# Running two attention mixers inside the input projection of block 2 of a two-block transformer kernel

## The reference

```python
def token_mixer_2(h, w_in, w_out, lam_params, subln_gain, layer):
    proj = h @ w_in                                   # (512,1024) @ (1024,3072)
    qa, ka, va, qb, kb, vb, qc, kc, vc = jnp.split(proj, idx, axis=-1)
    o_a = dilated_attention(...)        # 6 heads of 64: softmax(q k^T + bias) v
    o_b = differential_attention(...)   # 4 heads: (softmax(q1 k1^T + b) - lam softmax(q2 k2^T + b)) v, q/k of 32
    o_b = rmsnorm(o_b, subln_gain) * (1.0 - lam_init)
    o_c = stick_breaking_attention(...) # 6 heads
    mixed = jnp.concatenate([from_heads(o_a), from_heads(o_b), from_heads(o_c)], axis=-1)
    return mixed @ w_out
```

## Time and profile before

| what | value |
|---|---|
| median of 3 runs | 3406.91 us |
| range of the runs | 3401.34 to 3408.74 us |
| span of the profiled execution | 3402.8 us |
| PE busy | 3190.5 us (94%) |
| projection to end of attention with z(0), z(1), layer 0 | 1688.59 to 1905.28 us |
| the same, layer 1 | 2724.97 to 2940.14 us |

### The profile page before, as it was taken

How to read it: one execution, slowest core, us unless ns; L and a number is a source line. 1 busy time by engine, 2 the same in 40 slices (tenths; PEclk the granted TensorE clock), 3 DMA queues, 4 the chain that set the end, 5 groups by cost and what they waited for, 6 DMA issues and landing times.

```text
span 3402.8 us, 61162 instructions
## 1 busy us (share of the span) xinstructions
PE 3190.5 (94%) x26588; PEld 2518.9 (74%) x26588; DVE 1893.5 (56%) x2803; ACT 1251.0 (37%) x2065; POOL 179.8 (5%) x168
## 2 busy tenths in 40 slices
PE   7989789999997889999998899999999999899999
PEld 6866678865532335998886579988998886579987
DVE  4457566565221116884426568845885424658853
ACT  3227434321100003543324654534443324654432
POOL 0013222131000000000000000000000000000000
PEclk9999899999999999999999999999999999999999
DMA  7140000224999994333430023332332331013322
GB/s 264 50 161 11 3 4 3 71 80 173 408 413 421 421 421 162 103 97 112 136 118 13 1 87 100 100 112 87 112 102 99 133 119 38 1 62 112 100 93 87
DMA packets 179765, 441.65 MB, mean 130 GB/s; under 512 B 7602, under 2 KB 107692, under 8 KB 154924
## 3 DMA queue, kind: packets, MB, share of 16 engines
q1 hardware_dynamic: 179500, 437.74, 34.8%
HBM read 435.62 MB, written 2.10 MB: 129 GB/s over the span
## 4 chain that ended last, share of the span: by engine, by line
PE 72%; DMA 8%; DVE 7%; ACT 4%; issue 3%; POOL 0%; SPq 0%; ACTq 0%; DVEq 0%; POOLq 0%
PE banks L349 8%; PE banks L3616 7%; PE banks L3619 7%; PE banks L3618 7%; PE banks L2733 5%; PE banks L3737 4%; PE banks L3738 4%; PE banks L3736 4%; DMA ring<-in_exp_w_down 3%; DMA ring<-in_exp_w_gate 3%; DMA ring<-in_exp_w_up 1%; PE banks L973 1%; PE banks L957 1%; PE banks L911 1%; PE banks L393 1%
## 5 line engine op out<-in xcount | busy, mean ns | idle before, releaser
L2733 PE MATMUL banks<-ring,arena 128*64 128x512 f32 x1120 | 263.0, 606 | 37.8 <-DMA ring<-in_exp_w_gate 13.8
L3738 PE MATMUL banks<-tail_r,hid_r 128*128 128x512 f32 x704 | 279.7, 397 | 0.0
L3737 PE MATMUL banks<-ring_r,two_r 128*128 128x512 f32 x640 | 254.1, 397 | 0.0
L3736 PE MATMUL banks<-tail_r,two_r 128*128 128x512 f32 x640 | 250.7, 392 | 0.0
L2733 PEld LDWEIGHTS banks<-ring,arena 128*64 128x64 f32 x1120 | 86.4, 139 | 201.1 <-issue 186.8
L3616 PE MATMUL banks<-ring_r,tail_r 128*128 128x256 f32 x624 | 175.6, 281 | 9.0 <-DVE arena L3701 9.0
L304 DVE TENSOR_TENSOR hid_r<-arena,two_r 128x1024 fp32r<-128x1024 f32 x40 | 49.0, 1226 | 238.1 <-ACT two_r L301 223.8
L3618 PE MATMUL banks<-ring_r,tail_r 128*128 128x256 f32 x624 | 175.9, 282 | 0.0
L3616 PE MATMUL banks<-mix_r,tail_r 128*128 128x256 f32 x624 | 175.5, 281 | 0.0
L3618 PE MATMUL banks<-h_r,tail_r 128*128 128x256 f32 x624 | 174.7, 280 | 0.0
L3619 PE MATMUL banks<-mix_r,ring_r 128*128 128x256 f32 x608 | 171.1, 281 | 0.0
(11 more groups left out here) (587 smaller groups left out, 8685.1 us busy)
## 6 DMA issues: line engine op xcount, KB each, us to landing
ring<-in_exp_w_gate SPq DMA_DIRECT2D x62, 1024.0 KB, 23.0
ring<-in_w_ffn_gate SPq DMA_DIRECT2D x44, 1024.0 KB, 5.3
ring<-in_w_ffn_up SPq DMA_DIRECT2D x44, 1024.0 KB, 5.4
ring<-in_exp_w_down SPq DMA_DIRECT2D x40, 1024.0 KB, 23.0
ring<-in_w_ffn_down SPq DMA_DIRECT2D x20, 2048.0 KB, 7.9
ring<-in_exp_w_up SPq DMA_DIRECT2D x38, 1024.0 KB, 20.0
ring<-in_w_in SPq DMA_DIRECT2D x13, 2048.0 KB, 10.1
arena<-in_exp_w_up SPq DMA_DIRECT2D x26, 1024.0 KB, 23.5
```

The costliest lines, as they stand in the source:

```text
L2733: ins = TE.matmul(banks[64 * e:64 * e + 64, b0 + hf, :], lhs(kk, e), w[:, k, hf * 512:(hf + 1) * 512], start=(kk == 0), stop=(kk == KD - 1))
L3736: TE.matmul(bank, h_hi, w_hi[:, c, ns], start=(f == 0), stop=False)
L3737: TE.matmul(bank, h_hi, w_lo[:, c, ns], start=False, stop=False)
L3738: ins = TE.matmul(bank, h_lo, w_hi[:, c, ns], start=False, stop=(f == NF - 1))
```

## The change: what it does

The stages `products`, dilated and differential `attention` of a mixer become one stage with a function for each engine (`w_pe`, `w_act`, `w_dve`). The matmuls, the splits, the softmax operations and their sizes are the same. What differs:

- Groups 0 to 3 (query and key columns of the first heads) come first in banks 0 to 3. The other 24 groups are cut into pieces. Round k of PE (k from -1 to 21) is: `scores(k+1)`, piece (k,0), `turn(k-1)`, piece (k,1), `values(k-2)`, piece (k,2).
- Attention takes banks 0 to 3 for scores, 4 and 5 for turning, 7 for values. So the projection's groups, from the fifth on, all use bank 6 (`bank_of`; one of them, group 5, uses bank 7). A group can begin only when ACT has copied the one before out of bank 6 (`read`).
- ACT alone copies the groups out. In its round k it does: the copy of groups ended in piece (k-1,2), the splits due there, `weights(2k+2)`, `normal(2k+1)`, the copy of groups ended in (k,0), the splits due, `evac(k-1)`, `weights(2k+3)`, `normal(2k+2)`, the copy of groups ended in (k,1), the splits due, `out_`. DVE has its half of the splits at the same three places: between `unit(2k+2)` and `unit(2k+3)`, and behind each.
- The identity matmuls are gone.
- The units are taken in another order and have their high halves at other places (`homes`); the last two weight transfers are issued later, behind the biases, into ring slots 1 and 2, since slot 0 holds the softmax tiles.
- The results of the two attentions go to `qk` instead of `mixT` (which still holds the projection's input), and the output projection splits them from there in five parts instead of four.

How the pieces fall is decided by the planner in the code (`share`, `must`, `chunks`). Its answer for the rounds that have the most to them, as group and matmuls of its 24 (`qk11 20-24` are the last four of the group for row block 11 of `qk`; `+u15` says that unit 15 is split there):

| round: scores made | piece 0 | piece 1 | piece 2 |
|---|---|---|---|
| 2: dilated, t=3 | v0.2 22-24, v0.3 0-10 | v0.3 10-22 | v0.3 22-24, qk4 0-24 |
| 3: dilated, t=0 | none | none | none |
| 9: dilated, t=2 | qk8 13-20 | qk8 20-24 | qk9 0-10 +u10 +u11 |
| 10: dilated, t=3 | qk9 10-19 | qk9 19-24 | v384.0 0-24 |
| 13: differential, t=2 | qk10 7-19 | qk10 19-24, qk11 0-7 +u14 | qk11 7-20 |
| 14: differential, t=3 | qk11 20-24, qk12 0-11 +u15 | qk12 11-24 | qk13 0-19 +u16 |
| 15: differential, t=0 | qk13 19-24 | qk14 0-5 +u17 | qk14 5-10 |
| 16: differential, t=1 | qk14 10-18 | qk14 18-24 | qk15 0-10 |
| 17: differential, t=2 | qk15 10-21 | qk15 21-24, v640.0 0-12 | v640.0 12-24 |
| 18: differential, t=3 | v640.1 0-24 | v640.2 0-22 | v640.2 22-24, v640.3 0-19 |

The core of the diff:

```diff
-                            gs.append({"by": halves(len(gs)), "loads": [n], "read": read, "unit": u,
+                            gs.append({"loads": n, "read": read, "unit": u, "cost": 1.0,
...
+                    OPEN = 4
...
+                            split_at.setdefault(first_of[max(u - 2, 0 if before_ is None else before_ + 1)], []).append(u)
+                    bank_of = lambda i: i if i < OPEN else 7 if i == OPEN + 1 else 6
...
+                    def share(k, r):
+                        size = lambda j: (1 if j < DIL else 2) * width(steps[j][2]) if 0 <= j < N else 0
+                        inner = 0.5 + 0.0011 * (size(k + 1) + size(k - 1) + size(k - 2)) / 2
+                        return max(0.8, r * (0.9 + 0.0042 * size(k + 1)) - inner) / 0.2326
...
+                    def beside(l, k, c):
+
+                        if (k, c) not in chunks:
+                            return
+                        if l is act:
+                            for i in ended(k, c):
+                                group_out(l, i)
+                        for i in begun_in(k, c):
+                            for u in split_at.get(i, ()):
+                                split_unit(l, u)
...
+                                l.wait_ge(ring_full[g["loads"][0] % RING], g["loads"][1])
+                                l.wait_ge(*past(nm, "lo", g["unit"]))
+                                if i > OPEN and bank_of(i) == 6:
+                                    l.wait_ge(*past(nm, "read", i - 1 if bank_of(i - 1) == 6 else i - 2))
...
+                        for k in range(-1, N + 2):
+                            if k + 1 < N:
+                                scores(k + 1)
+                            elif k == N:
+                                z(l, 0)
+                            fill(k, 0)
+                            if 1 <= k <= N:
+                                turn(k - 1)
+                            fill(k, 1)
+                            if k >= 2:
+                                values(k - 2)
+                            fill(k, 2)
...
+                        for k in range(-1, N + 2):
+                            beside(l, k - 1, 2)
+                            if k + 1 < N:
+                                weights(2 * k + 2)
+                            normal(2 * k + 1)
+                            beside(l, k, 0)
+                            evac(k - 1)
+                            if k + 1 < N:
+                                weights(2 * k + 3)
+                            normal(2 * k + 2)
+                            beside(l, k, 1)
...
+                        def unit(u):
+                            if u < 2 * N:
+                                biased(u)
+                            if 0 <= u - 2 < 2 * DIL:
+                                finish(u - 2)
+                            if 2 * DIL <= u - 3 < 2 * N:
+                                finish(u - 3)
+                            if u < 2 * N:
+                                highest(u)
+                            if 1 <= u <= 2 * N:
+                                inverse(u - 1)
...
+                        for k in range(-1, N + 1):
+                            beside(l, k - 1, 2)
+                            unit(2 * k + 2)
+                            beside(l, k, 0)
+                            unit(2 * k + 3)
+                            beside(l, k, 1)
...
-                    dil_scores, dil_last = next(dil)
-                    gs[28]["behind"] = dil_scores
-                    gs[30]["by"], gs[31]["by"] = "act", None
-                    products(nm, gs, units=units, fence=False, presplit=1, begun=(2, early))
...
-                    next(dil, None)
-                    slot_user[ws[4][0][0] % RING] = (di, "turned", 11, 1)
-                    next(dif, None)
+                    stage(nm, fence=False, pe=w_pe, act=w_act, dve=w_dve)
```

More of the change, by code:

```diff
@@ L3803, in mixer @@
                         cut = lambda ap, o=o, width=width: ap[:, :, o:o + width]
-                        hi = ffn_r(ytmp_at + 11264 if u == 0 else extra if u % 2 else rest_end, KD, width)
+                        hi = (ring_r if hi_at < RING_WORDS else ffn_r)(hi_at, KD, width)
                         lo = cut(ring_r(at_, KD, whole_))
+                        unit_of[c0] = (len(units), lo, hi)
+                        if c0 == 0:
+                            unit_of[c0 + P] = (0, lo[:, :, P:2 * P], hi[:, :, P:2 * P])
                         units.append((cut(region(at_, KD, whole_)), lo, hi, n))
-                        unit_of[c0] = (u, lo, hi)
-                        if c0 == 0:
-                            unit_of[c0 + P] = (u, lo[:, :, P:2 * P], hi[:, :, P:2 * P])
-                    assert len(units) % 2 == 0, "the last unit, the widest, needs the larger buffer"
-                    gs = []
-                    for c0 in sorted(list(fm) + list(tm)):
+                    gs, group_of = [], {}
+                    for c0 in [c for c0, _ in unit_cols for c in ((0, P) if c0 == 0 else (c0,))]:
                         n = chunk_of[c0][0]
@@ L3834, in mixer @@
                                 ts = slice(t * P, (t + 1) * P)
-                                gs.append({"by": halves(len(gs)), "loads": [n], "unit": u,
+                                group_of["v", v0, t] = len(gs)
+                                gs.append({"loads": n, "unit": u, "cost": {384: 0.757, 256: 0.509}[width],
                                            "read": copy_out(vt[:, t, v0:v0 + width], lambda b, width=width: b[:, 0:width]),
@@ L3845, in mixer @@
                     small(nm + "bias", [(b_dil[i], a["k_bias"][i, :, 0:T]) for i in range(6)], after=f"mid{l_}a")
-                    pt = region(base.at + 4 * D, 2, 2 * NT, P)
                     b_dif = region(rest_end, 4, T)
+                    small(nm + "bias2", [(b_dif, a["k_bias"][6:10, :, 0:T].rearrange("h p n -> p h n"))], when=[(nm, "used", 2)])
+                    n_loads[0] = first + 5
+                    for p in pieces[4:]:
+                        got, _ = stream_many([((KD, w_), w_src[:, :, c_:c_ + w_]) for c_, w_ in p])
+                        assert got == chunk_of[p[0][0]][0]
+                    n_loads[0] = first + 9
                     width = lambda t: P * (t + 1)
@@ new lines, in mixer @@
+                    chunks, at_g, at_m, due = {}, OPEN, 0, 0.0
+                    for k in range(-1, N + 2):
+                        for c in range(3):
+                            here = chunks[k, c] = []
+                            if k < N:
+                                due += share(k, hi_r) / 3
+                            while at_g < len(gs):
+                                forced = c == 2 and (at_g <= must.get(k + 1, -1) or k >= N - 1)
+                                g = gs[at_g]
+                                take = len(g["mms"]) - at_m if forced else min(len(g["mms"]) - at_m, int(due / g["cost"] + 0.5))
+                                if take <= 0:
+                                    break
+                                here.append((at_g, at_m, at_m + take))
+                                due -= take * g["cost"]
+                                at_m += take
+                                if at_m == len(g["mms"]):
+                                    at_g, at_m = at_g + 1, 0
+                                    if not forced and due < 6:
+                                        break
@@ new lines, in mixer, with split_unit @@
+                    assert at_g == len(gs)
+                    ended = lambda k, c: [i for i, _, j in chunks[k, c] if j == len(gs[i]["mms"])]
+                    begun_in = lambda k, c: [i for i, j, _ in chunks[k, c] if j == 0]
+                    def split_unit(l, u):
+                        x_, lo, hi, n = units[u]
+                        if l is act:
+                            l.wait_ge(ring_full[n[0] % RING], n[1])
+                            if homes[u][1] is not None:
+                                l.wait_ge(*past(nm, "used", homes[u][1]))
+                            l.did(S.activation(hi, x_, ACT.Copy).then_inc(l.sem, 1), nm, "hi", u)
+                        else:
+                            l.wait_ge(*past(nm, "hi", u))
+                            l.did(V.tensor_tensor(lo, x_, hi, ALU.subtract).then_inc(l.sem, 1), nm, "lo", u)
@@ L3936, in mixer @@
-                    dif_scores, _ = next(dif)
-                    sb_at = ws[4][0][0] % RING * SLOT
-                    dil = attention(di, ((0, 1), (2, 3), (4, 5)), width, s_dil, lambda h, j: vt[:, j, h * HD:(h + 1) * HD],
-                                    lambda pair: [(mixT[:, pair[0] // 2, :], slice(0, P))], HD ** -0.5,
-                                    ([region(sb_at + i * T, T) for i in range(6)], pt, stats[:, 64:112].rearrange("p (a b) -> p a b", b=8)),
-                                    bias=lambda h, t: b_dil[h][:, 384 - P * t:T], need=(nm + "bias",), ahead_of=dif_scores,
```

(3 more changed lines are left out.)

305 lines of the change are left out of this document (245 added, 60 removed).

## The result

The changed kernel takes 3418.14 us (median of 8 runs, 3412.26 to 3424.74), the kernel before on the same chip 3405.83 us (3397.28 to 3410.41). The ratio is 1.0036, 95% interval 1.0025 to 1.0047: slower by 0.36%. Forecast were 3394 us and "faster"; the time lies inside the range of 3358 to 3423, on the other side of no change.

The account below looks back on a forecast made before the run. Projection was taken as bound by PE, attention as a chain through DVE and ACT; 71 us gained, less 51 of new waits and 8 of slow clock, took 12 us off 3406.9: 3395 us (middle 3394), range 3358 to 3423.

Parts of the forecast that it names:

- The gains: In both mixers' attention, the waits and identity matmuls to be removed, with smaller items: 71 us in all.
- the fillers: Identity matmuls in the mixers' attention: removing them was to save 18.3 us in layer 0 and 17.5 us in layer 1.
- the waits of attention: PE's idle time in attention: removing it was to save 15.0 us in layer 0 and 14.8 us in layer 1.
- the wait for the value unit's split: PE's wait for the wide value unit, to go because its split comes two groups earlier: 1.7 us a layer.
- The walked waits: New PE waits in the mixers, priced by stepping PE, DVE and ACT through the rounds: 25.5 us a layer, 51 us.
- round 14 piece 0: PE waits to begin qk12 until ACT, behind the round's softmax, has copied qk11 out of bank 6: 3.8 us.
- the turning behind unit 17: Round 15's turning waits for DVE, which is held by the split of the 3072 wide unit: 3.65 us.
- The clock: PE slowed to 1.2 GHz after long waits in the mixers: 4 us a layer, 8 us.
- The bound that I set: Limits for the slow clock's cost: nothing, or 3.4 us for each of five.
- The pieces' edges: Switches between projection and attention matmuls: no cost taken; scores, turnings and value products were to cost PE the same.
- The prediction's own sign for the slow side: In the profile after, waits and slow stretches over 35.5 us a layer would show the forecast wrong as too fast.
- the fourth: Slower: each of five waits over 2 us a layer brings 6.8 us at 1.2 GHz; 3421 us, chance 0.23.

Follow-up runs that it names:

- the right-dosed fillers: The changed kernel plus identity matmuls that fill some nine tenths of its seven longest waits in a mixer: 3404.95 us, ratio 0.9993.
- the fastest version: The changed kernel with ACT's copy ahead of exponentials, also behind piece 1 in rounds 10, 11, 14, and unit 17 split in three parts: 3368.36 us, ratio 0.9890.

## Why the prediction was wrong

Summed over both mixers, 419.9 us were forecast (431.9 - 71 + 51 + 8) and 444.0 came. That the time still lies inside the range says nothing for the account: the forecast was faster, and the range reached far to the slow side. By its terms:

- **The gains came as reckoned**: the fillers are gone, the waits of attention and the wait for the value unit's split too. But the fillers had a use that the sum gave no price, as the kernel before without them shows.
- **The walked waits, 51 us: 57.3 measured.** Large ones, walked and measured: round 14 piece 0 3.8 and 4.33; the turning behind unit 17 3.65 and 3.04; round 17 2.8 and 3.32; round 10 piece 2 2.7 and 2.65; round 13 2.2 and 2.61; round 2 1.9 and 2.46. Missed were the turning of round 4 (1.53) and most of round 11 (1.92 for 0.5); round 14 piece 2 was 0.41 for 1.3, round 16 piece 2 nothing for 1.8. 6.3 us short. The way of reading was right.
- **The clock, 8 us: 19 measured. This is the step that failed**: "I take 4 us a layer, since PE's lateness shortens the waits that follow". PE's busy time after was 386.7 us; the version that makes the same matmuls in 54 runs at PEclk 1.00 throughout has 367.6, so 19 us of work are the clock's. In time the right-dosed fillers give back 13.6 us by the windows and 14.6 by the ratios; the remainder turns into waits. The bound that I set (3.4 us for each of five) would have held it. I took the wait of 2.81 us in the earlier trace rows that was followed by no slow stretch as a sign that waits of that length are free. It was one case, at another place of the program, and the walk had three waits of 2.2 to 2.8 us in each layer beside the two longer ones. Of the changed kernel's twelve waits of 2.4 us and more ten have a slow stretch beside them.
- **The pieces' edges, nothing: some 7 us measured** (367.6 against 360.8 of work forecast at full clock). The prediction said that scores, turnings and value products "cost PE the same between pieces as behind the projection"; they got cheaper (44.6 us a layer in the fastest version, where 51.5 were left in the sum for layer 0), but the projection, which the sum took over unchanged, rose from 129.3 to 139.3 us in 54 runs, 0.19 us for each.

6.3 + 11 + 6.8 = 24.1 us, the whole difference. The clock is the largest of the three, but no one of them gives the sign: with 19 us for the clock and all else as forecast the sum is 3406.9 - 71 + 51 + 19 = 3406, no change; the short walk and the pieces' edges make it slower. The prediction's own sign for the slow side, waits and slow stretches of over 35.5 us a layer, came true: 28.4 and 28.9 us of waits and, at most, 13.6 and 8.5 us of lost full speed. Outside the mixers 0.5 us is left: a longer slow stretch in layer 0's stick-breaking (10.2 us for 3.4) against a first block that ended 2.9 us earlier in this execution. Of the rivals the fourth was right in mechanism and sign and too dear in its price; it took five stretches of 6.8 us a layer, and there were six and four, seven of the ten only 3.4 us long. The rule of the Trainium skill named in the prediction (TensorE: Matmul & The Clock Gate, "A second HAM failure mode: psum-queue depth-cycling") is that frequent small idle stretches of PE between groups of matmuls can make its clock go up and down. The traces agree that it goes up and down at the hand-overs; but in the changed kernel and its variants no slow stretch begins beside a wait under 1.8 us, and only some of the waits of 1.8 to 2.7 us have one. The page gives no length, and that every larger hand-over costs a slow stretch was the prediction's reading of it.

What stays open: why layer 1, with the same waits to 0.02 us in most places, had 17 us at 1.2 GHz and layer 0 27. No run tells it. Open too is how the slow stretches lay in the executions that were not profiled.

## What to carry to other kernels

When matmuls of one product are laid between the steps of a chain, the bank that they share is handed over by whichever engine copies it out, and that copy must stand in its engine's list where the engine is idle, ahead of what waits for the chain: moving one instruction was worth 0.7% here, and moving it in three more rounds with one wide split cut up another 0.8%, which turned 0.36% slower into 1.1% faster. Price a wait of a dense matmul stream with the slow clock behind it, and before fillers are called waste, take them out alone. What a clock costs in work is more than what mending it gives in time (19 and 14 us here), since the next wait grows. Fill a wait, if at all, by the instructions as the trace counts them.

## What the runs showed of the hardware

All waits of PE of at least 0.8 us in the mixers of the changed kernel and of its eleven variants, both layers (those at a mixer's first matmul left out), and whether a stretch at 1.2 GHz began in the wait or within 1.5 us behind it:

| wait | how many | beside a stretch at 1.2 GHz |
|---|---|---|
| 0.8 to 1.7 us | 82 | none |
| 1.8 to 2.3 us | 24 | 10 (some lie in pairs and can't be told apart) |
| 2.4 to 2.7 us | 13 | 8 |
| 2.8 to 4.4 us | 27 | 27 |

The same wait (2.46 us in round 2) was followed by one in layer 0 and by none in layer 1. The stretches lasted 3.4, 6.8 or 10.2 us. In the mixers of the kernel before without fillers, whose waits are no longer than 2.85 us, they ran to 37.5 and 30.7 us at a time. The table holds for the changed kernel and its variants alone: in the attention of the kernel before, stretches began beside waits of 1.48 us (1860.01, layer 0) and 1.07 us (2926.30, layer 1), and without its fillers beside one of 1.40 us (2902.25). So the length of a wait alone does not decide it, and no run here tells what else does.

A switch between a run of projection matmuls and one of attention has a price too. PE in order of time in the fastest version, at such a place:

```profile
1814.27 0.40 PE L4008 MATMUL banks<-mix_r,ffn_r 128*128 128x512 f32 x1
1814.51 0.39 PE L4008 MATMUL banks<-h_r,ffn_r 128*128 128x512 f32 x1
1814.83 1.14 PE L4041 MATMUL banks<-arena 32*128 32x512 f32 x8
1815.90 0.50 PE L4008 MATMUL banks<-mix_r,ring_r 128*128 128x512 f32 x1
1816.24 0.39 PE L4008 MATMUL banks<-mix_r,ffn_r 128*128 128x512 f32 x1
1816.47 0.39 PE L4008 MATMUL banks<-h_r,ffn_r 128*128 128x512 f32 x1
```

The pitch is 0.23 us inside the run, but 0.32 from its last matmul to the scores and 0.34 from the next run's first matmul to its second. No wait lies there, and it is 0.2 us for this run; over the whole projection of a layer it is 10 us.
